# Decay sums of a gated recurrence: two levels in one product of 256 columns, with two sets of decayed queries and keys

## The chip, the cores and the metric

One core of one Trainium2 chip runs the whole kernel. The metric is the device time of one execution in microseconds (us). The kernel before took 1091.51 us, the median of 3 runs (1090.42 to 1091.56).

## The reference, cut to what matters

The program is two transformer blocks over 256 positions of width 1024: first attention with a retention branch and a feed-forward part, then a second block with a feed-forward part, a mixing part, cross attention to a memory, and another feed-forward part. Everything is float32. The change lies in the mixing part of the second block, in its gated recurrence (HGRN2) of 4 heads of 128 channels:

```python
def step(state, inp):                       # one chunk of positions
    qi, ki, vi, bi = inp                    # bi = cumulative sum of log f
    diff = bi[:, :, :, None, :] - bi[:, :, None, :, :]
    decay = jnp.exp(jnp.where(causal, diff, -jnp.inf))
    scores = jnp.einsum('bhtk,bhsk,bhtsk->bhts', qi, ki, decay)
    o = jnp.einsum('bhts,bhsv->bhtv', scores, vi) + \
        jnp.einsum('bhtk,bhkv->bhtv', qi * jnp.exp(bi), state)
    ...
```

With log f the logarithm of the forget gate, the score of position t with an earlier position s is the sum over the 128 channels of q[t] k[s] exp(sum of log f from s+1 to t). Beside it the mixing part projects its input to seven pieces of 512 columns (zf, zq, zi, zc, zu, zb, zg), convolves zc*zu over the positions, multiplies by zb, and projects both results back (w_out).

## The kernel before, in words

**Products of the projections.** TensorE rounds float32 operands in its fast mode, so every weight and every input is split into a high and a low part (w_hi, w_lo, hT_hi, hT_lo), and each product is three (function `three`, lines 1661 to 1663). The weights come in units of 128 x 2048. A unit passes through three rings of 3 slots: SyncE loads it (raw), ScalarE copies the high part (L583, `split_to`), VectorE subtracts to get the low part (L1056, `low_to`), TensorE uses it (`unit`: 24 products of 512 columns). ScalarE's copy waits until TensorE has used the unit three before it.

**The recurrence by levels.** The 256 positions are two blocks of 128. Inside a block the pairs (s, t) are sorted into 7 levels: at level l the block is cut into segments of 2^(l+1) positions, and the pairs with s in the early half and t in the late half of one segment belong to level l (LEVELS = 7). An eighth step, level 7, gives the pairs across the two blocks. For every level:

1. TensorE sums log f from each position to the middle of its segment: a product of logf_hi and logf_lo (128 positions x 128 channels, stationary) with a 0/1 matrix of 128 columns (`sums_r`, one matrix for each level), for 4 heads and 2 blocks: `decay_sums(level)`, L2073 and L2074. Block 0 goes to PSUM bank 4, block 1 to bank 7.
2. ScalarE takes the exponential into one of two buffers, `qk_dec[level % 2]` (the halves of `xn`): `level_decays(level)`, L949, 2 instructions of 128x512. The buffer is free when the pair scores of two levels ago have been made.
3. VectorE multiplies the late halves by the queries and the early halves by the keys: `decayed(level)`, L1541.
4. TensorE multiplies every head's 128x128 tile with itself: `pair_scores(level)`, L2092, 8 products. At level 7 it is 4 products into one bank ("cross", L2084).
5. VectorE keeps the pairs of this level by a mask: `keep_pairs`, L1529.

**The order of the work.** Each engine's order is written out by hand. On TensorE it is: transposes of queries and keys (L2063), `decay_sums(0)`, the pairs of a position with itself ("diag", L2114, 8 products), and then 8 steps. Step n computes unit n of the eight units of zc, zu, zb and zg, then `decay_sums(n + 1)`, then `pair_scores(n)`. At the end of step 5 it transposes zc*zu ("uT", L2100, into banks 2 and 3, which hold zb until ScalarE has copied it out), at the end of step 6 zb ("bT", the same line and banks). In the middle of step 7 stand the cross products. Then come the products with the values (L2143, L2146) and w_out, whose first half needs `conv_lo`, the low part of the convolution's result (L1594).

ScalarE's order here is: copies of the transposed queries (L963) and keys (L967), two weight copies, the zi piece (`streamed_out`, L646), and then in each of steps 0 to 7 one weight copy, `level_decays(step)` and what else is due: zc in step 1, zb in step 5, uT in step 6 (L983). After that come the two high parts of the convolution (L989), a weight copy, zg, and so on. VectorE in each level waits for both exponentials, runs `decayed`, `keep_pairs` of the level before, and a `low_to`; after level 6 comes the convolution (L1558, L1562), after level 7 the product with zb (L1569), the copy of the cross scores (L1581), a `low_to` and `conv_lo` (L1594).

**Banks.** `BankPlan` gives every use of a PSUM bank a name, in the order of use: `streamed` or `signalled` puts a fill on the list of its bank. `free(engine, name)` waits until every earlier fill of the bank has been read; `filled` waits until this one is written; `read_out` waits until this one has been read.

Of the kernel before, what the change touches and what calls it, by code (L numbers as in the profile page):

```python
# [32 lines left out]
ACT = mybir.ActivationFunctionType  # L33
AX = mybir.AxisListType

P = 128
# [157 lines left out]
def plan_banks():  # L194
# [85 lines left out]
    transposes("hkT", 2)  # L280
    for blk in range(TB):
        plan.signalled(("diag", blk), 5 + blk)
    for level in range(LEVELS):
        for blk in range(TB):
            plan.signalled(("decay", level, blk), [4, 7][blk])
            plan.signalled(("pairs", level, blk), 5 + blk)
        for step, name in ((LEVELS - 2, "uT"), (LEVELS - 1, "bT")):
            if level == step:
                plan.signalled(f"{name}0", 2)
                plan.signalled(f"{name}1", 3)  # L290
    for blk in range(TB):
        plan.signalled(("decay", LEVELS, blk), [4, 7][blk])
    plan.signalled("cross", 5)
    for blk in range(TB):
        plan.signalled(("hgrn", blk), [4, 7][blk])
# [26 lines left out]
def two_blocks_kernel(nc, io):  # L322
# [10 lines left out]
    with sems, stack:  # L333
# [122 lines left out]
        scT = carve(at, 8 * P); at += 1024  # L456
        crossT = carve(at, 4 * P); at += 512
        head_row = rows[:, 1, 0:512]
        lb_p = carve(at, 2, 512); lb = carve(at + 1024, 512); one_lb = carve(at + 1536, 512); at += 2048
        hgrn_sq = [lb_p[:, blk, :] for blk in range(TB)]  # L460
        level_mask = const2[:, (LEVELS + 2) * P:].rearrange("p (l t) -> p l t", t=P)
        qk_dec = [xn[:, b, :] for b in range(2)]


        mq = carve(0, TB, D)
# [21 lines left out]
        def filled(eng, name):  # L487

            b, _, s = plan.of[name]
            eng.wait_ge(bank_full[b], s + 1)  # L490
            return bank[b]

        def read_out(eng, name):

            b, k, _ = plan.of[name]
            eng.wait_ge(bank_read[b], k + 1)
# [7 lines left out]
        def read_sem(name):  # L504
            return bank_read[plan.of[name][0]]
# [72 lines left out]
        def _(act):  # L578
# [361 lines left out]
                for tb in range(TB):  # L940
                    copy_out((part, tb), dst[:, tb, :], func, scale=rstd[:, tb:tb + 1])

            def level_decays(level):
                for blk in range(TB):
                    b = filled(act, ("decay", level, blk))
                    if blk == 0 and level >= 2:

                        filled(act, ("pairs", level - 2, 1))
                    act.activation(qk_dec[level % 2][:, blk * 512:(blk + 1) * 512], b[:, :], ACT.Exp)\  # L949
                        .then_inc(read_sem(("decay", level, blk)), 1)  # L950

            streamed_out(0, "zf", fgate, ACT.Sigmoid)
            act.wait_ge(sem("fgate"), 1)
# [16 lines left out]
            for step in range(8):  # L970
                if step < LEVELS:
                    split_to(W_IN2 + 6 + step + RING)
                level_decays(step)
                if step == 1:
                    streamed_out(3, "zc", zc_sb)
                if step == 3:
                    split_to(W_IN2 + 10 + RING)
                if step == 5:
                    streamed_out(5, "zb", zb_sb)
                if step == LEVELS - 1:  # L980
                    for j in range(2):
                        b = filled(act, f"uT{j}")
                        act.activation(uT.rearrange("p (c t) -> p c t", t=T + 2)[:, 2 * j:2 * j + 2, 2:T + 2],  # L983
                                       b[:, :].rearrange("p (c t) -> p c t", t=T), ACT.Copy).then_inc(read_sem(f"uT{j}"), 1)
# [55 lines left out]
        def _(dve):  # L1040
# [490 lines left out]

            def decayed(level):

                buf = qk_dec[level % 2]
                for late, other in ((1, hqT), (0, hkT)):
                    h = 1 << level
                    v = buf.rearrange("p (n two h) -> p n two h", two=2, h=h)[:, :, late, :] if level < LEVELS else \
                        buf[:, late * 512:late * 512 + 512]
                    o = other.rearrange("p (n two h) -> p n two h", two=2, h=h)[:, :, late, :] if level < LEVELS else \
                        other[:, late * 512:late * 512 + 512]  # L1540
                    ins = dve.tensor_tensor(v, v, o, ALU.mult)  # L1541
                ins.then_inc(sem("level_decayed"), 1)
# [27 lines left out]
                                      b[:, :].rearrange("p (c t) -> p c t", t=T), ALU.mult).then_inc(read_sem(f"bT{j}"), 1)  # L1570

            for level in range(LEVELS + 1):
                read_out(dve, ("decay", level, 0))
                read_out(dve, ("decay", level, 1))
                decayed(level)
                if level:
                    keep_pairs(level - 1, ("pairs", level - 1))
                if level == LEVELS:
                    gated_convolution()
                    b = filled(dve, "cross")  # L1580
                    dve.tensor_copy(crossT, b[:, :]).then_inc(read_sem("cross"), 1)  # L1581
                low_to(W_IN2 + 9 + level)
                if level == LEVELS - 1:
                    convolution()
                if level == 4:

                    dve.wait_ge(split_used, W_IN2 + 10)
                    read_out(dve, ("zc", 1))
                    for tb in range(TB):
                        dve.scalar_tensor_tensor(out=zc_sb[:, tb, :], in0=bank_of(("zu", tb))[:, :], scalar=rstd[:, tb:tb + 1],  # L1590
                                                 in1=zc_sb[:, tb, :], op0=ALU.mult, op1=ALU.mult).then_inc(read_sem(("zu", tb)), 1)
# [66 lines left out]
        def _(pe):  # L1658
# [404 lines left out]
                        ins = pe.transpose(b[:, h * P:(h + 1) * P], src[:, blk, h * P:(h + 1) * P], ident)  # L2063
                    ins.then_inc(full_sem((name, blk)), 1)

            def decay_sums(level):

                for blk in range(TB):
                    b = free(pe, ("decay", level, blk))
                    m = sums_r[:, level + blk if level == LEVELS else level, :]  # L2070
                    for h in range(HG_HEADS):
                        o = b[:, h * P:(h + 1) * P]
                        pe.matmul(o, logf_hi[:, blk, h * P:(h + 1) * P], m, start=True, stop=False)  # L2073
                        ins = pe.matmul(o, logf_lo[:, blk, h * P:(h + 1) * P], m, start=False, stop=True)  # L2074
                    ins.then_inc(full_sem(("decay", level, blk)), 1)

            def pair_scores(level):

                pe.wait_ge(sem("level_decayed"), level + 1)
                buf = qk_dec[level % 2]  # L2080
                if level == LEVELS:
                    b = free(pe, "cross")
                    for h in range(HG_HEADS):
                        ins = pe.matmul(b[:, h * P:(h + 1) * P], buf[:, h * P:(h + 1) * P],  # L2084
                                        buf[:, 512 + h * P:512 + (h + 1) * P], start=True, stop=True)
                    ins.then_inc(full_sem("cross"), 1)
                    return
                for blk in range(TB):
                    b = free(pe, ("pairs", level, blk))
                    for h in range(HG_HEADS):  # L2090
                        v = buf[:, blk * 512 + h * P:blk * 512 + (h + 1) * P]
                        ins = pe.matmul(b[:, h * P:(h + 1) * P], v, v, start=True, stop=True)  # L2092
                    ins.then_inc(full_sem(("pairs", level, blk)), 1)
# [9 lines left out]

            pe.wait_ge(sem("sums_ready"), 1)
            pe.wait_ge(sem("logf_lo"), 1)
            decay_sums(0)
            for name in ("hqT", "hkT"):
                for q in range(2):
                    read_out(pe, (name, q))
            for blk in range(TB):  # L2110
                b = free(pe, ("diag", blk))
                for h in range(HG_HEADS):
                    s = slice(blk * 512 + h * P, blk * 512 + (h + 1) * P)
                    ins = pe.matmul(b[:, h * P:(h + 1) * P], hkT[:, s], hqT[:, s], start=True, stop=True)  # L2114
                ins.then_inc(full_sem(("diag", blk)), 1)
            parts = ["zc", "zu", "zb", "zg"]
            for step in range(8):
                k, half = step // 2, step % 2
                v = W_IN2 + 6 + step
                if half == 0:  # L2120
                    outs = [free(pe, (parts[k], tb)) for tb in range(TB)]
                h = 1 - half if parts[k] == "zg" else half
                unit(v, v + 1, [(hT_hi, hT_lo, tb, outs[tb]) for tb in range(TB)], range(4 * h, 4 * h + 4), 512,
                     half == 0, half == 1, {1: lambda: pair_scores(LEVELS)} if step == LEVELS else {})
                if step < LEVELS:
                    decay_sums(step + 1)
                    pair_scores(step)

                if step == LEVELS - 2:
                    read_out(pe, ("zu", 1))  # L2130
                    positions_last("uT", zc_sb)
                if step == LEVELS - 1:
                    read_out(pe, ("zb", 1))
                    positions_last("bT", zb_sb)
# [173 lines left out]
```

## Time and profile before

| | |
|---|---|
| median of 3 runs | 1091.51 us (1090.42 to 1091.56) |
| profiled execution | 1091.91 us, its span 1090.1 us |
| TensorE (PE) busy | 1035.2 us, 95% |
| VectorE (DVE) busy | 603.1 us, 55% |
| ScalarE (ACT) busy | 490.9 us, 45% |
| chain that ended last | PE 86%, DVE 7%, DMA 3%, ACT 2% |

The span runs from the first to the last profiled instruction. PEld is TensorE's weight load, which can lie beside a running product. The duration printed for one product includes its way through the array, so the pace of a row of products is read from the distance between their starts. "Idle before" is time in which the engine of the row did nothing just ahead of it, with what ended that.

### The profile page before, as it was taken

What the parts mean: (1) busy time and instruction counts of PE and PEld (TensorE: products, weight loads), DVE (VectorE), ACT (ScalarE), POOL (GpSimd) and SP (SyncE); (2) the same over time, 40 slices, a digit from 0 to 9 for tenths busy, and PEclk for the clock granted to TensorE, in tenths of its full rate; (3) what the DMA queues carried; (4) which work ended last, traced back from release to release, by engine and by line L of the source; (5) the groups of instructions that cost most, each with busy time, mean ns of one, the idle gap of its engine ahead of it and who ended that gap; (6) DMA issues with size and microseconds to landing.
All of it is one profiled execution on the core that took longest, in us unless ns stands there. A gap on an engine that the chain in (4) does not pass through costs nothing.

```text
span 1090.1 us, 13384 instructions
## 1 busy us (share of the span) xinstructions
PE 1035.2 (95%) x5212; PEld 843.4 (77%) x5212; DVE 603.1 (55%) x706; ACT 490.9 (45%) x581; POOL 0.2 (0%) x4
## 2 busy tenths in 40 slices
PE   4699999999999999999999999999999799999996
PEld 1477768887788888888888887788877578888885
DVE  1572665576755554475555545756775345555543
ACT  3343445536643444364444434653545335444531
POOL 0000000000000000000000000000000000000000
PEclk9799999999999999999999999999999899999998
DMA  9766473213455555545555555433235126545540
GB/s 373 282 237 260 171 298 117 78 40 114 177 175 194 188 188 188 192 176 204 191 188 189 171 193 216 174 136 116 88 144 193 39 78 230 175 173 192 193 155 38
DMA packets 26543, 188.71 MB, mean 173 GB/s; under 512 B 2945, under 2 KB 3201, under 8 KB 3969
## 3 DMA queue, kind: packets, MB, share of 16 engines
q1 hardware_dynamic: 25920, 185.63, 46.8%
q10 hardware_dynamic: 576, 2.43, 0.6%
q8 instruction: 34, 0.56, 0.2%
q14 instruction: 13, 0.10, 0.0%
HBM read 187.00 MB, written 1.05 MB: 173 GB/s over the span
## 4 chain that ended last, share of the span: by engine, by line
PE 86%; DVE 7%; DMA 3%; ACT 2%; issue 1%; SPq 0%; DVEq 0%; ACTq 0%
PE bank L1661 24%; PE bank L1663 24%; PE bank L1662 24%; DMA raw<-in_weights 3%; DVE w_lo L1056 2%; PE bank L1728 2%; PE bank L1889 1%; PE bank L1998 1%; PE bank L1717 1%; PE bank L1878 1%; ACT w_hi L583 1%; PE bank L2184 1%; PE bank L2092 1%; PE bank L2193 1%; PE bank L1928 1%
## 5 line engine op out<-in xcount | busy, mean ns | idle before, releaser
L1056 DVE TENSOR_TENSOR w_lo<-raw,w_hi 128x2048 fp32r<-128x2048 f32 (+1 forms) x151 | 338.9, 2248 | 278.2 <-ACT w_hi L583 278.1
L583 ACT ACTIVATE w_hi<-raw 128x2048 fp32r<-128x2048 f32 x148 | 283.1, 1916 | 277.6 <-PE bank L1663 249.6
L1661 PE MATMUL bank<-w_hi,hT_hi 128*128 128x512 f32 (+1 forms) x864 | 342.7, 397 | 5.7 <-issue 3.0
L1663 PE MATMUL bank<-w_hi,hT_lo 128*128 128x512 f32 (+1 forms) x864 | 336.8, 390 | 0.0
L1662 PE MATMUL bank<-w_lo,hT_hi 128*128 128x512 f32 (+1 forms) x864 | 336.3, 389 | 0.0
L1661 PEld LDWEIGHTS bank<-w_hi,hT_hi 128*128 128x128 f32 x864 | 163.4, 189 | 47.2 <-issue 9.6
L1663 PEld LDWEIGHTS bank<-w_hi,hT_lo 128*128 128x128 f32 x864 | 163.1, 189 | 34.4
L1662 PEld LDWEIGHTS bank<-w_lo,hT_hi 128*128 128x128 f32 x864 | 163.5, 189 | 32.1 <-issue 0.2
L1661 PE MATMUL bank<-w_hi,gT_hi 128*128 128x512 f32 x264 | 103.3, 391 | 0.0
L1663 PE MATMUL bank<-w_hi,gT_lo 128*128 128x512 f32 x264 | 102.8, 389 | 0.0
L1662 PE MATMUL bank<-w_lo,gT_hi 128*128 128x512 f32 x264 | 102.7, 389 | 0.0
L1663 PEld LDWEIGHTS bank<-w_hi,gT_lo 128*128 128x128 f32 x264 | 49.6, 188 | 10.4
L1662 PEld LDWEIGHTS bank<-w_lo,gT_hi 128*128 128x128 f32 x264 | 49.6, 188 | 10.2
L1661 PEld LDWEIGHTS bank<-w_hi,gT_hi 128*128 128x128 f32 x264 | 49.6, 188 | 10.0
L1728 PE MATMUL bank<-raw,silu_c 128*32 128x512 f32 x192 | 29.5, 715 | 19.7 <-DMA raw<-in_weights 19.7
L858 ACT ACTIVATE arena<-bank,rstd 128x256 f32<-128x256 f32 x44 | 18.4, 470 | 63.5 <-PE bank L1663 63.5
L1455 DVE SCALAR_TENSOR_TENSOR arena<-bank,rstd,arena 128x256 f32<-128x256 f32 x44 | 19.3, 479 | 30.8 <-ACT arena L858 30.8
L1728 PEld LDWEIGHTS bank<-raw,silu_c 128*32 128x32 f32 x192 | 4.7, 116 | 33.6 <-DMA raw<-in_weights 19.4
L1297 DVE TENSOR_REDUCE row_max<-bank 128x1 f32<-128x512 f32 (+1 forms) x24 | 14.4, 602 | 24.3 <-PE bank L1878 16.3
L1661 PE MATMUL bank<-memT_hi,w_hi 128*128 128x256 f32 x64 | 26.4, 412 | 0.0
L1443 DVE SCALAR_TENSOR_TENSOR x_res<-bank,x_res 128x512 f32<-128x512 f32 x16 | 10.3, 686 | 26.7 <-PE bank L1663 26.7
L1461 DVE TENSOR_TENSOR gT_lo<-bank,gT_hi 128x512 f32 (+1 forms) x33 | 22.8, 690 | 3.2
(261 smaller groups left out, 993.3 us busy)
## 6 DMA issues: line engine op xcount, KB each, us to landing
raw<-in_weights SPq DMA_DIRECT2D x172, 1024.0 KB, 4.7
arena<-in_const ACTq DMA_DIRECT2D x1, 1088.0 KB, 5.0
x_res<-in_x SPq DMA_DIRECT2D x1, 1024.0 KB, 8.3
arena<-in_ctx SPq DMA_DIRECT2D x1, 1024.0 KB, 9.9
memKT<-in_mem SPq DMA_DIRECT2D x1, 1024.0 KB, 10.3
out<-xn SPq DMA_DIRECT2D x2, 512.0 KB, 2.7
arena<-in_const SPq DMA_DIRECT2D x1, 770.0 KB, 6.3
rows<-in_final_norm ACTq DMA_DIRECT2D x1, 512.0 KB, 5.1
```

Source lines behind the costliest of these rows:

```text
L583: act.activation(w_hi[:, v_slot, :], raw[:, u_slot, :], ACT.Copy).then_inc(hi_ready, 1)
L858: act.activation(gate[:, c % 3, tb, :], bank[(c % 3) * 2 + tb][:, 0:256], ACT.Silu, scale=rstd[:, tb:tb + 1] if f else 1.0)\
L1056: ins = dve.tensor_tensor(w_lo[:, v_slot, n], raw[:, u_slot, n], w_hi[:, v_slot, n].bitcast(F32), ALU.subtract)
L1297: chain(dve.reduce_max(row_max[:, s:s + 1], b[:, 0:n], AX.X))
L1455: dve.scalar_tensor_tensor(out=g, in0=bank[b][:, 256:512], scalar=rstd[:, tb:tb + 1] if f else 1.0, in1=g, op0=ALU.mult, op1=ALU.mult).the ...
L1461: dve.tensor_tensor(gT_lo[:, s, :], bank[6][:, :].rearrange("p (a t) -> p a t", t=T), gT_hi[:, s, :].bitcast(F32), ALU.subtract).then_inc( ...
L1661: pe.matmul(out, hi, rhi, start=start, stop=False)
L1662: pe.matmul(out, hi, rlo, start=False, stop=False)
L1663: return pe.matmul(out, lo, rhi, start=False, stop=stop)
L1717: ins = pe.transpose(b[:, e * T + tb * P:e * T + (tb + 1) * P], src[:, tb, (2 * q + e) * P:(2 * q + e + 1) * P], ident)
L1728: ins = pe.matmul(b[32 * j:32 * j + 32, :], silu_c[:, k, :], raw[:, u % RING, 512 * j:512 * j + 512], start=(k == 0), stop=(k == MOD_K - 1))
L1878: pe.matmul(b[:, :], qaT[:, j, tb * P:(tb + 1) * P], kaT[:, kv, :], start=True, stop=True).then_inc(full_sem(("scores", s)), 1)
```

## The change

Eight times 16 products of 128 columns become eight times 8 products of 256 columns: two neighbouring matrices of `sums_r` are the moving operand of one product. `decay_sums(p, blk)` now makes the sums of levels 2p and 2p+1 of one block, two heads in each bank (bank 4 for heads 0 and 1, bank 7 for heads 2 and 3). The second set of decayed queries and keys (`dec_set`) lies in the arena where the bounds of the forget gate lay; each set holds two levels.

```diff
+    for p in range((LEVELS + 1) // 2):
+        for blk in range(TB):
+            for hp in range(2):
+                plan.signalled(("decay", p, blk, hp), [4, 7][hp])
     for level in range(LEVELS):
         for blk in range(TB):
-            plan.signalled(("decay", level, blk), [4, 7][blk])
             plan.signalled(("pairs", level, blk), 5 + blk)
...
-    for blk in range(TB):
-        plan.signalled(("decay", LEVELS, blk), [4, 7][blk])
...
-        lb_p = carve(at, 2, 512); lb = carve(at + 1024, 512); one_lb = carve(at + 1536, 512); at += 2048
+        dec_set = carve(at, 2, 1024); lb_p = carve(at, 2, 512); lb = carve(at + 1024, 512); one_lb = carve(at + 1536, 512); at += 2048
...
-        qk_dec = [xn[:, b, :] for b in range(2)]
+        dec_sets = [xn[:], dec_set]
+        qk_dec = lambda level: dec_sets[level // 2 % 2][:, level % 2, :]
...
-            def level_decays(level):
-                for blk in range(TB):
-                    b = filled(act, ("decay", level, blk))
-                    if blk == 0 and level >= 2:
-
-                        filled(act, ("pairs", level - 2, 1))
-                    act.activation(qk_dec[level % 2][:, blk * 512:(blk + 1) * 512], b[:, :], ACT.Exp)\
-                        .then_inc(read_sem(("decay", level, blk)), 1)
+            def level_decays(p, blk):
+                for hp in range(2):
+                    b = filled(act, ("decay", p, blk, hp))
+                    if blk == 0 and hp == 0 and p >= 2:
+                        filled(act, ("pairs", 2 * p - 3, 1))
+                    at = blk * 512 + hp * 256
+                    act.activation(dec_sets[p % 2][:, :, at:at + 256].rearrange("p l (h t) -> p h l t", t=P),
+                                   b[:, :].rearrange("p (h l t) -> p h l t", l=2, t=P), ACT.Exp)\
+                        .then_inc(read_sem(("decay", p, blk, hp)), 1)
...
-                level_decays(step)
+                if step == 0:
+                    level_decays(0, 0)
+                    level_decays(0, 1)
+                elif step < LEVELS:
+                    level_decays((step + 1) // 2, (step - 1) % 2)
...
-                read_out(dve, ("decay", level, 0))
-                read_out(dve, ("decay", level, 1))
+                if level % 2 == 0:
+                    for blk in range(TB):
+                        for hp in range(2):
+                            read_out(dve, ("decay", level // 2, blk, hp))
...
-            def decay_sums(level):
-
-                for blk in range(TB):
-                    b = free(pe, ("decay", level, blk))
-                    m = sums_r[:, level + blk if level == LEVELS else level, :]
-                    for h in range(HG_HEADS):
-                        o = b[:, h * P:(h + 1) * P]
-                        pe.matmul(o, logf_hi[:, blk, h * P:(h + 1) * P], m, start=True, stop=False)
-                        ins = pe.matmul(o, logf_lo[:, blk, h * P:(h + 1) * P], m, start=False, stop=True)
-                    ins.then_inc(full_sem(("decay", level, blk)), 1)
+            def decay_sums(p, blk):
+
+                m = sums_r[:, 2 * p:2 * p + 2, :]
+                if 2 * p + 1 == LEVELS and blk:
+                    m = sums_r[:, 2 * p:2 * p + 3:2, :]
+                for hp in range(2):
+                    b = free(pe, ("decay", p, blk, hp))
+                    for e in range(2):
+                        o = b[:, e * 2 * P:(e + 1) * 2 * P].rearrange("p (l t) -> p l t", t=P)
+                        d = slice((2 * hp + e) * P, (2 * hp + e + 1) * P)
+                        pe.matmul(o, logf_hi[:, blk, d], m, start=True, stop=False)
+                        ins = pe.matmul(o, logf_lo[:, blk, d], m, start=False, stop=True)
+                    ins.then_inc(full_sem(("decay", p, blk, hp)), 1)
...
-            decay_sums(0)
+            decay_sums(0, 0)
             for name in ("hqT", "hkT"):
...
                 ins.then_inc(full_sem(("diag", blk)), 1)
+            decay_sums(0, 1)
...
                 if step < LEVELS:
-                    decay_sums(step + 1)
+                    if step < LEVELS - 1:
+                        decay_sums((step + 2) // 2, step % 2)
                     pair_scores(step)
```

## Rows read from the trace of the kernel before

**Rows 1.** The page: busy time of the engines, and the chain of waits by engine.
```profile
PE 1035.2 (95%) x5212; PEld 843.4 (77%) x5212; DVE 603.1 (55%) x706; ACT 490.9 (45%) x581; POOL 0.2 (0%) x4
PE 86%; DVE 7%; DMA 3%; ACT 2%; issue 1%; SPq 0%; DVEq 0%; ACTq 0%
```
**Rows 2.** Groups of instructions by line and form: the decay sums.
```profile
L2074 PE MATMUL bank<-sums_r,logf_lo 128*128 128x128 f32 x64 | 14.7, 276 | 0.0
L2073 PE MATMUL bank<-sums_r,logf_hi 128*128 128x128 f32 x64 | 14.4, 268 | 0.0
```
**Rows 3.** Timeline of TensorE: start, duration (us), instruction, count.
```profile
710.92 0.31 PE L2073 MATMUL bank<-sums_r,logf_hi 128*128 128x128 f32 x1
...
712.74 2.00 PE L2114 MATMUL bank<-arena 128*128 128x128 f32 x16
714.49 0.48 PE L1661 MATMUL bank<-w_hi,hT_hi 128*128 128x512 f32 x1
...
720.02 0.22 PE L2073 MATMUL bank<-sums_r,logf_hi 128*128 128x128 f32 x1
...
721.76 2.00 PE L2092 MATMUL bank<-xn 128*128 128x128 f32 x16
...
765.39 0.22 PE L2073 MATMUL bank<-sums_r,logf_hi 128*128 128x128 f32 x1
```
**Rows 4.** Timeline of TensorE where products of 256 columns run in a row.
```profile
162.08 0.28 PE L1661 MATMUL bank<-memT_hi,w_hi 128*128 128x256 f32 x1
...
162.44 0.28 PE L1661 MATMUL bank<-memT_hi,w_hi 128*128 128x256 f32 x1
```
**Rows 5.** Timeline of ScalarE around the first exponentials.
```profile
710.71 1.09 ACT L967 ACTIVATE arena<-bank 128x512 f32<-128x512 f32 x2 [0.26 <-PE bank L2063]
711.69 3.71 ACT L583 ACTIVATE w_hi<-raw 128x2048 fp32r<-128x2048 f32 x2
715.30 1.26 ACT L646 ACTIVATE arena<-bank,rstd 128x512 f32<-128x512 f32 x2
716.57 1.28 ACT L949 ACT_TABLE_LOAD   x1
717.87 1.09 ACT L949 ACTIVATE xn<-bank 128x512 f32<-128x512 f32 x2
```
**Rows 6.** Timeline of ScalarE and VectorE from unit 5's end to w_out.
```profile
765.65 1.91 ACT L583 ACTIVATE w_hi<-raw 128x2048 fp32r<-128x2048 f32 x1 [6.19 <-PE bank L1663]
767.47 1.25 ACT L646 ACTIVATE arena<-bank,rstd 128x512 f32<-128x512 f32 x2
...
769.79 1.30 DVE L1541 TENSOR_TENSOR xn<-xn,arena 128x512 f32<-128x512 f32 x2 [5.51 <-ACT xn L949]
...
779.43 1.29 DVE L1541 TENSOR_TENSOR xn<-xn,arena 128x512 f32<-128x512 f32 x2
...
782.58 1.23 ACT L989 ACTIVATE hT_hi<-arena 128x512 fp32r<-128x512 f32 x2 [3.20 <-DVE arena L1569]
783.71 1.90 ACT L583 ACTIVATE w_hi<-raw 128x2048 fp32r<-128x2048 f32 x1
...
787.85 1.29 DVE L1594 TENSOR_TENSOR hT_lo<-arena,hT_hi 128x512 fp32r<-128x512 f32 x2
```
**Rows 7.** Timeline of TensorE: the cross products and the start of w_out.
```profile
782.56 1.05 PE L2084 MATMUL bank<-xn 128*128 128x128 f32 x8
...
789.20 0.50 PE L1661 MATMUL bank<-w_hi,hT_hi 128*128 128x512 f32 x1 [0.16 <-DVE hT_lo L1594]
```
**Rows 8.** Windows: busy time and count by engine, granted clock, DMA share, GB/s.
```profile
284.00:288.00 4.00, 2.24 (x10) 1.58 (x9) 3.78 (x8) 1.65 (x3) 0.00 (x0) 1.00 0.61 246
...
668.00:672.00 4.00, 3.09 (x22) 2.40 (x20) 1.87 (x4) 1.45 (x5) 0.00 (x0) 1.00 0.47 133
672.00:676.00 4.00, 2.82 (x7) 2.28 (x8) 4.00 (x8) 2.61 (x7) 0.00 (x0) 0.69 0.85 342
676.00:680.00 4.00, 4.00 (x17) 3.27 (x16) 2.15 (x4) 1.69 (x2) 0.00 (x0) 0.89 0.51 145
```

More of the change, by code:

```diff
@@ L1532, in decayed @@
             def decayed(level):
-                buf = qk_dec[level % 2]
+                buf = qk_dec(level)
                 for late, other in ((1, hqT), (0, hkT)):
@@ L2064, in _ @@
                     ins.then_inc(full_sem((name, blk)), 1)
-            def decay_sums(level):
-                for blk in range(TB):
-                    b = free(pe, ("decay", level, blk))
-                    m = sums_r[:, level + blk if level == LEVELS else level, :]
-                    for h in range(HG_HEADS):
-                        o = b[:, h * P:(h + 1) * P]
-                        pe.matmul(o, logf_hi[:, blk, h * P:(h + 1) * P], m, start=True, stop=False)
-                        ins = pe.matmul(o, logf_lo[:, blk, h * P:(h + 1) * P], m, start=False, stop=True)
-                    ins.then_inc(full_sem(("decay", level, blk)), 1)
+            def decay_sums(p, blk):
[10 more added lines that the diff above has]
+                    ins.then_inc(full_sem(("decay", p, blk, hp)), 1)
             def pair_scores(level):
                 pe.wait_ge(sem("level_decayed"), level + 1)
-                buf = qk_dec[level % 2]
+                buf = qk_dec(level)
                 if level == LEVELS:
```

## The prediction

> **What bounds the kernel.** I read the page first, then the groups by line, then the timelines of the stretch that the change touches. TensorE is busy for 1035.2 us of the 1090.1 us span and makes up 86% of the chain that ended last [rows 1]. So a microsecond taken off TensorE's queue is a microsecond off the time, unless TensorE then waits for something. The whole question is where in this stretch it would wait, and the timelines answer it. The profiled execution took 1091.91 us, 0.4 above the median of the runs shown (1091.51). I sum against the first and take 0.4 off at the end.
>
> **What the decay sums cost now.** They are 128 products (64 and 64) [rows 2]. Their printed durations overlap, so I take distances between starts. After unit 0, 16 of them stand between 720.02 and the pair scores at 721.76: 1.74 us, about 0.11 each. The first group takes 1.82 (710.92 to 712.74) [rows 3]. TensorE doesn't pause between them, so all eight groups, 1.82 + 7 x 1.74 = 14.0 us, are on its queue.
>
> **What they cost after.** 64 products of 256 columns. Such products run elsewhere in this kernel: three of them between 162.08 and 162.44, 0.12 each [rows 4]. A group of 8 is then 0.96 us, and each group saves 0.78. Bounds for the new product: not below the 0.11 of the one with half the columns (group 0.88, saving 0.86), and not above 0.23, the product of 512 columns, which is 24 in a unit: 714.49 to 720.02 is 5.53 us [rows 3] (group 1.84, saving -0.10). The row of the same width decides, 0.96. The one group whose moving operand is two matrices with a third between them has no row of its own; it comes behind unit 5 and, as shown below, does not count.
>
> The Trainium skill ("TensorE: Matmul & The Clock Gate", section "Back-to-back issue gap") gives about 81 ns for one product of 128 columns in a stream with its weight loads and about 131 ns for 512. An estimate from that page for 256 columns, on a straight line between, is 98 ns; a group would go from 1.30 to 0.78 us and save 0.51. The trace has 110 and 230 ns for the two ends [rows 3], so the measurement disagrees and decides.
>
> **The start: a new wait.** This is the step that matters most. Before, level 0's two blocks went to banks 4 and 7, and both banks were free. Now block 0 fills both banks (heads 0 and 1, heads 2 and 3), and block 1 needs both again. `decay_sums(0, 1)` stands on TensorE's queue ahead of unit 0, and `free` makes it wait until ScalarE has taken the exponential of block 0 out of bank 4. When is that? ScalarE's queue before its first exponential holds the key copies, two weight copies (711.69, 3.71 us), zi (715.30) and a table load (716.57); the first exponential starts at 717.87 [rows 5]. None of these waits for anything that the change brings forward: they run back to back. Two exponentials take 1.09 us, the first alone 0.6, so bank 4 is read at about 718.5 and bank 7 at 719.0.
>
> TensorE's side: block 0 from 710.92 takes 0.96 and the first group's extra 0.08, to 711.95. The diagonal products need the key copies, which end at 711.80 (710.71 + 1.09), so they hardly wait; they take 1.75 (712.74 to 714.49) and end at about 713.7. Then TensorE stands still until 718.5, for 4.8 us. Four products into bank 4, then four into bank 7, which is free at 719.0: unit 0 starts at about 719.5 in place of 714.49 [rows 3, 5]. That is 5.0 us late, and everything behind it on the queue (unit 0, all pair scores, all later units) is late with it.
>
> Bounds of this wait: if the exponential, which now writes four runs of 128 in place of one of 512, keeps its time, it is 5.0. The nearest row is the same instruction with the plain layout; I see no reason for a gain, and if a run cost it half as much again, bank 7 would be free 0.5 later, so 5.0 to 5.5. I take 5.0.
>
> **Steps 0 to 4.** Behind each of units 0 to 4 a group of 8 replaces one of 16: 5 x 0.78 = 3.9 us won. On the new times no wait comes due here. Pair scores of level 0 need the exponentials of both blocks (to about 720.4) and 1.3 us of VectorE; TensorE asks for them when unit 0 and a group have passed, 719.5 + 5.5 + 1.0 = 726.0. Not late. From there on ScalarE's exponentials of one block follow each group as before, two 128x512 instructions in each step, and VectorE's two levels come from sums that are complete one step earlier or at the same step as before. Before unit 5 nothing gets late.
>
> So unit 5 ends at 765.39 + 5.0 - 3.9 = 766.5, that is 1.1 us later than now.
>
> **From unit 5's end to w_out: nothing is won.** Behind it two groups go (the one of level 7 wholly, another one halved), 1.74 + 0.78 = 2.5 us of TensorE's queue. But w_out starts at 789.20, after a wait for the low part of the convolution [rows 7], and that comes from a chain of ScalarE and VectorE which begins at unit 5's end: weight copy 765.65, zb 767.47, exponentials, VectorE's `decayed` at 769.79, mask, low part, convolution, `decayed` of level 7 at 779.43, product with zb, ScalarE's high parts at 782.58, weight copy 783.71, VectorE's low part, and the low part of the convolution at 787.85 [rows 6]. From 765.39 to 789.20 it is 23.8 us with hardly a gap, and the change leaves every instruction of it where it is (two exponentials behind zb, as now). TensorE will wait inside this stretch. The transposes of zc*zu need the banks of zb, read out at 768.72 (3.3 behind unit 5's end), and TensorE comes there after 0.96 + 1.75 = 2.7: 0.6 of waiting. The cross products need `decayed` of level 7, done at 780.72, 15.3 behind; they start now at 782.56, 17.2 behind [rows 6, 7]. The remaining 2.1 us or so are waited before w_out. So w_out starts 1.1 us late as well, and the rest of the kernel, whose order is the same, shifts by 1.1.
>
> **The clock.** Where TensorE did little before 673, the granted clock fell: 1.00, then a mean of 0.69 and of 0.89 over two stretches of 4 us [rows 8]. Its levels are full (2.4 GHz) and half (1.2 GHz), so it was half for (0.31 + 0.11) x 4 x 2 = 3.4 us, which cost TensorE about 1.7 us of work. In the stretch 668 to 672 TensorE was still busy for 3.09 of 4 us, and 2.82 of the next 4. The new wait of 4.8 us without any product is a longer pause than any there. I expect the clock to fall once and take 1.7 us. Bounds: 0 (it stays up), and 3.4 (twice as long at half).
>
> The Trainium skill ("TensorE: Matmul & The Clock Gate", section "HAM oscillation — how this bites in real kernels") says that a wait between two bursts of products throws the gate back to half rate, and that the fall is paid at every such wait. By it the time is the 1.7 us case. The trace agrees with it around 673 and not at 284 to 288 [rows 8]. By the rule alone the second new pause, of 2.1 us before w_out, would be a risk too.
>
> **Sum.** 1091.91 + 5.0 - 3.9 + 0 + 1.7 = 1094.7; less 0.4 for the median: 1094.3 us, slower by 0.26%.
>
> **The rivals.**
>
> *The clock stays up.* The same without the 1.7: 1092.6. For it: between 284 and 288 TensorE was idle for about 1.8 of 4 us and the clock stayed at 1.00 [rows 8], so not every pause is punished. Against: that pause is much shorter than 4.8 us. It would count as no change.
>
> *It falls twice.* The pause before w_out (2.1 us, behind light products of 128 columns) brings a second fall, or the first lasts longer: 1094.3 + 1.7 = 1096.0. For it: around 673, where the clock fell, the pauses were no longer. Against: the one at 284 to 288 is about as long and cost nothing [rows 8].
>
> *No new wait at the start.* If banks 4 and 7 were free for block 1, because ScalarE reads them earlier, unit 0 would start at about 714.7 and the pair scores of level 0 would wait 0.4 for four exponentials in a row. Then 0.6 - 3.9 = -3.3 us, 1088.2: faster. The decision falls at 713.7: the first exponential would have to end by then, 4.8 us sooner than now, and the table load and zi ahead of it stand in [rows 5]. Nothing in the trace shows this.
>
> *TensorE's work is all that counts.* Then 14.0 - 8 x 0.96 = 6.3 us are won, 1085.2. Against: both waits above, of the new one and that of [rows 6].
>
> *The 256-column products are slow.* Group 1.84: nothing won, and 5.0 + 0.5 + 1.7 late: 1098.7. Against: [rows 4].
>
> **Chances.** Forecast (new wait, one fall of the clock) 0.50; clock stays up 0.20; two falls 0.17; no wait or TensorE alone 0.08; slow products or later exponentials 0.05. A measurement of this kernel tells a change from none at about 0.2%, which is 2.2 us: slower begins at 1093.7. The forecast lies 0.6 us beyond it, and as the length of the half-rate stretch varies, about a quarter of its chance ends below. So slower: 0.37 + 0.17 + 0.05 = 0.59; same: 0.13 + 0.20 = 0.33; faster: 0.08. The range takes in the clock's bounds and both neighbours, 1091.6 to 1096.8; it leaves out the faster cases, the slow products and the corners.
>
> **What would show each step.** In the new trace: TensorE idle for 4.8 us between the diagonal products and the second group of sums, released by ScalarE's first exponential; unit 0 starting near 719.5; products of sums 0.12 apart; unit 5's end near 766.5 plus the clock's share; the distance from there to the start of w_out 23.8 us, with idle time of TensorE at the transposes of zc*zu, the cross products and w_out; a granted clock of 0.5 just after 718. The prediction is wrong if unit 0 starts near 714.7, if the distance of 23.8 shrinks, or if the clock holds.

## The result and the profile after

The changed kernel took 1094.69 us (median of 6 runs, 1092.64 to 1096.5), the kernel before 1091.24 (6 runs, 1089.76 to 1091.56): ratio 1.0030, 95% interval 1.0018 to 1.0042. A second set (12 runs of the changed kernel, 29 of the kernel before) gave 1093.95 against 1090.55, ratio 1.0030 (1.0018 to 1.0043). One execution in the experiments below was disturbed (5886 us) and is left out of its median. Slower by 0.3%, though TensorE has 5.3 us less to do (1035.2 in [rows 1], 1029.9 now). Below, times inside the stretch are counted from the first product of the decay sums, since the two profiled executions reach it 0.24 us apart (710.92 and 710.68).

The page of the kernel after, busy time and the chain by engine; and the row of granted clock in 40 slices, which for the kernel before was `9799999999999999999999999999999899999998`:

```profile
PE 1029.9 (94%) x5148; PEld 837.0 (77%) x5148; DVE 602.7 (55%) x706; ACT 490.8 (45%) x581; POOL 0.2 (0%) x4
...
PEclk9799999999999999999999999999999999999999
...
PE 85%; DVE 7%; ACT 3%; DMA 3%; issue 1%; SPq 0%; DVEq 0%; ACTq 0%
```

ScalarE's part of the chain rose from 2% to 3%. The groups by line and form answer to [rows 2]: half the products, twice the columns, and a wait of 4.4 us that wasn't there.

```profile
L2085 PE MATMUL bank<-sums_r,logf_hi 128*128 128x256 f32 x32 | 8.9, 306 | 4.4 <-ACT xn L951 4.4
L2086 PE MATMUL bank<-sums_r,logf_lo 128*128 128x256 f32 x32 | 8.7, 299 | 0.0
```

TensorE's timeline after, answering to [rows 3] and [rows 7]:

```profile
710.68 0.36 PE L2085 MATMUL bank<-sums_r,logf_hi 128*128 128x256 f32 x1
...
711.81 2.02 PE L2126 MATMUL bank<-arena 128*128 128x128 f32 x16
718.27 0.58 PE L2085 MATMUL bank<-sums_r,logf_hi 128*128 128x256 f32 x1 [4.44 <-ACT xn L951]
...
720.15 0.63 PE L1670 MATMUL bank<-w_hi,hT_hi 128*128 128x512 f32 x1
...
726.12 0.28 PE L2085 MATMUL bank<-sums_r,logf_hi 128*128 128x256 f32 x1
...
727.07 1.95 PE L2104 MATMUL bank<-xn 128*128 128x128 f32 x16
...
767.24 0.28 PE L2085 MATMUL bank<-sums_r,logf_hi 128*128 128x256 f32 x1
...
783.60 1.13 PE L2096 MATMUL bank<-arena 128*128 128x128 f32 x8 [1.47 <-DVE arena L1536]
...
791.27 0.50 PE L1670 MATMUL bank<-w_hi,hT_hi 128*128 128x512 f32 x1 [1.11 <-DVE hT_lo L1603]
```

TensorE stands still behind the diagonal products until ScalarE has taken the exponential out of the bank. Unit 0 starts 9.47 us behind the first sums (720.15 - 710.68) where it was 3.57 [rows 3]. A group of sums takes 0.95 (726.12 to 727.07), and w_out starts at 80.59 in place of 78.28: 2.3 us late. ScalarE at the same place, answering to [rows 5]:

```profile
716.33 1.28 ACT L951 ACT_TABLE_LOAD   x1
717.62 1.08 ACT L951 ACTIVATE xn<-bank 128x512 f32<-128x512 f32 x2
719.53 0.60 ACT L951 ACTIVATE xn<-bank 128x512 f32<-128x512 f32 x1 [0.82 <-PE bank L2086]
720.39 0.60 ACT L951 ACTIVATE xn<-bank 128x512 f32<-128x512 f32 x1 [0.26 <-PE bank L2086]
```

An exponential with the new layout takes 0.60 us. One with the plain layout took as long in the kernel before:

```profile
776.38 0.60 ACT L949 ACTIVATE xn<-bank 128x512 f32<-128x512 f32 x1 [5.70 <-PE bank L2074]
```

The clock (windows, columns as in [rows 8]) fell in the wait:

```profile
712.00:716.00 4.00, 1.84 (x16) 1.64 (x15) 2.61 (x2) 4.00 (x4) 0.00 (x0) 1.00 0.00 0
716.00:720.00 4.00, 1.73 (x8) 1.73 (x9) 0.92 (x2) 3.15 (x5) 0.00 (x0) 0.72 0.75 262
720.00:724.00 4.00, 4.00 (x17) 3.29 (x17) 2.88 (x3) 0.73 (x2) 0.00 (x0) 0.85 0.02 4
```

From unit 5's end to w_out the chain of [rows 6] stands as it was: weight copy, zb, and at its end the high part of the convolution, two weight copies, and the low part:

```profile
767.50 1.91 ACT L585 ACTIVATE w_hi<-raw 128x2048 fp32r<-128x2048 f32 x1 [5.34 <-PE bank L1672]
769.32 1.25 ACT L648 ACTIVATE arena<-bank,rstd 128x512 f32<-128x512 f32 x2
...
784.66 1.23 ACT L996 ACTIVATE hT_hi<-arena 128x512 fp32r<-128x512 f32 x2 [10.63 <-DVE arena L1576]
785.80 3.70 ACT L585 ACTIVATE w_hi<-raw 128x2048 fp32r<-128x2048 f32 x2
...
789.93 1.28 DVE L1603 TENSOR_TENSOR hT_lo<-arena,hT_hi 128x512 fp32r<-128x512 f32 x2
```

It took 24.0 us (767.24 to 791.27) after 23.8 before.

The two profiled executions differ by 0.7 us only (1092.64 and 1091.91), less than the 2.3 by which w_out is late. The rows of granted clock show why: slice 32 (about 845 to 872 us) has 8 before and 9 after. The clock fell twice there in the profiled execution of before and once in that of after, and from w_out to the end it is 300.9 us before and 299.4 after. The second profile of the changed kernel has 8 in that slice and 300.4 us. Whether this goes with the kernel is open. All five profiles in which the clock stayed up through the first pause or had no such pause (before, filled wait, exponentials first, exponentials first with three moves, before with two moves) have 300.7 to 300.9 us behind w_out. Of the six in which it fell at the start, five have 299.1 to 299.4. So a fall at the start may be followed by one fall fewer here; no experiment tried that.

### The profile page after: what moved, and what is told of

It is laid out like the page before. It is cut to its first block, busy times and chain, and to the rows that moved or that the text cites. A ratio compares the mean times of both kernels' runs of the same rounds, so it can differ in the third digit from the quotient of the medians.

```text
span 1090.7 us, 13252 instructions
## 1 busy us (share of the span) xinstructions
PE 1029.9 (94%) x5148; PEld 837.0 (77%) x5148; DVE 602.7 (55%) x706; ACT 490.8 (45%) x581; POOL 0.2 (0%) x4
## 4 chain that ended last, share of the span: by engine, by line
PE 85%; DVE 7%; ACT 3%; DMA 3%; issue 1%; SPq 0%; DVEq 0%; ACTq 0%
PE bank L1670 24%; PE bank L1672 24%; PE bank L1671 24%; DMA raw<-in_weights 3%; DVE w_lo L1063 2%; PE bank L1737 2%; ACT w_hi L585 2%; PE bank L1898 1%; PE bank L2007 1%; PE bank L1726 1%; PE bank L1887 1%; PE bank L2104 1%; PE bank L2207 1%; PE bank L2198 1%; PE bank L1937 1%
```

## The experiments

Each was timed in five rounds beside the kernel before on the same chip; the groups of runs used different chips, so differences between two rows are best taken through each row's own time before. The last column of the table counts in each profile from the first decay sum to the start of w_out, which leaves out what the clock does elsewhere.

| kernel | median us | before us | ratio (95%) | to w_out |
|---|---|---|---|---|
| before | | | | 78.28 |
| changed | 1094.69 | 1091.24 | 1.0030 (1.0018 to 1.0042) | 80.59 |
| changed, again | 1093.95 | 1090.55 | 1.0030 (1.0018 to 1.0043) | 81.94 |
| wait alone | 1095.83 | 1090.86 | 1.0051 (1.0038 to 1.0065) | 83.77 |
| products of 128 | 1099.59 | 1090.86 | 1.0074 (1.0060 to 1.0088) | 85.86 |
| filled wait | 1091.57 | 1090.86 | 1.0004 (0.9995 to 1.0013) | 79.27 |
| exponentials first | 1086.81 | 1090.86 | 0.9962 (0.9949 to 0.9976) | |
| the same, again | 1088.20 | 1090.56 | 0.9977 (0.9963 to 0.9990) | 74.77 |
| two moves in the tail | 1093.00 | 1090.55 | 1.0021 (1.0012 to 1.0031) | 81.00 |
| three moves in the tail | 1090.52 | 1090.56 | 0.9999 (0.9985 to 1.0014) | 77.76 |
| exponentials first, three moves | 1085.05 | 1090.55 | 0.9945 (0.9930 to 0.9960) | 71.85 |
| before with two moves | 1090.64 | 1090.55 | 0.9996 (0.9987 to 1.0005) | 78.14 |

**The wait alone**, put into the kernel before:

```diff
+            read_out(pe, ("decay", 0, 0))
             parts = ["zc", "zu", "zb", "zg"]
```

> The kernel before with one more wait: TensorE, between the diagonal products and unit 0, waits until the exponential of level 0, block 0 has been taken. Theory A (the new wait at the start is what the change costs, and the clock falls in it): unit 0 starts at about 718.6 in place of 714.49, 4.1 us late, the clock falls once and takes about 1.4 more, nothing of it is made good later: 1091.2 + 5.5 = 1096.7 us. Rival B (a wait here is made good further on, and the change is slow for another reason, such as the wider products or the new layout of the exponentials): 1091 to 1092.

It came out as theory A has it: 5.0 us slower in the medians and 5.5 to w_out (83.77 - 78.28). Unit 0 starts 7.60 behind the first sums in place of 3.57, so 4.0 of this is the pause and 1.5 the slow clock. TensorE's waits in that profile hold one long entry, and nothing of it is made good on the way to w_out:

```profile
PE bank L1661 <- ACT xn L949: 3.8, 1, 3.8
```

**The products split**, in the changed kernel:

```diff
-                        pe.matmul(o, logf_hi[:, blk, d], m, start=True, stop=False)
-                        ins = pe.matmul(o, logf_lo[:, blk, d], m, start=False, stop=True)
+                        for l in range(2):
+                            pe.matmul(o[:, l, :], logf_hi[:, blk, d], m[:, l, :], start=True, stop=False)
+                            ins = pe.matmul(o[:, l, :], logf_lo[:, blk, d], m[:, l, :], start=False, stop=True)
```

> The changed kernel, each product of 256 columns made as two of 128 into the same places; every wait and bank as in the changed kernel. Theory A (a group of 16 takes 0.85 us more than one of 8, and only what stands ahead of unit 5's end counts): five groups behind units 0 to 4 and part of the group before unit 0, 5 x 0.85 + 0.6 = 4.9 us slower than the changed kernel, 1094.7 + 4.9 = 1099.6. Rival C (all of TensorE's work counts): 8 x 0.85 = 6.8 slower, 1101.5. Rival B (the wide products bring nothing): 1094.7.

1099.59, 4.9 above the changed kernel's 1094.69: what theory A names, and 1.9 short of rival C. Taken against each one's own time before, it is 5.3 (8.7 slower and 3.4 slower). To w_out it is 85.86, also 5.3 more than the first profile of the changed kernel. The groups behind unit 5 cost nothing: from unit 5's end to w_out it is 24.03 us with either width.

**The wait filled** with products, in the changed kernel:

```diff
+            spare = free(pe, ("zc", 0))
+            for _ in range(18):
+                pe.matmul(spare[:, :], hT_hi[:, 0, 0:P], hT_hi[:, 0:2, :].rearrange("p a t -> p (a t)"), start=True, stop=True)
             decay_sums(0, 1)
```

> The changed kernel with 18 products of 512 columns put into the wait ahead of the second group of sums, into a bank that unit 0 starts afresh; their result is not used. 18 x 0.23 = 4.1 us fit into the wait of 4.4. Theory A: the granted clock stays at 1.00 around 718, unit 0 starts about 0.9 earlier and runs at full pace, 1.4 us less than the changed kernel: 1093.3. Rival D (the clock's part is nothing, all of the loss is the pause): 1094.7, and the clock falls as well or its fall costs nothing.

TensorE's timeline in this kernel:

```profile
713.47 4.37 PE L2130 MATMUL bank<-hT_hi 128*128 128x512 f32 x18
718.15 0.38 PE L2085 MATMUL bank<-sums_r,logf_hi 128*128 128x256 f32 x1 [0.32 <-ACT xn L951]
...
719.22 0.40 PE L1670 MATMUL bank<-w_hi,hT_hi 128*128 128x512 f32 x1
```

Windows, columns as in [rows 8]:

```profile
716.00:720.00 4.00, 3.68 (x21) 2.90 (x20) 0.81 (x2) 3.63 (x6) 0.00 (x0) 1.00 0.74 262
720.00:724.00 4.00, 4.00 (x20) 3.30 (x19) 3.85 (x4) 0.02 (x1) 0.00 (x0) 1.00 0.00 0
```

The second group of sums starts at the same place (7.60 behind the first, 7.59 in the changed kernel), so the pause is as long; only the clock is different, and it stays up. To w_out it is 79.27: 1.3 less than the first profile of the changed kernel and 2.7 less than the second. The time fell by more than the expected 1.4: the ratio went from 1.0030 to 1.0004, some 2.8 us, though the two intervals leave room for half of that. In the second profile of the changed kernel the clock was at half for longer:

```profile
716.00:720.00 4.00, 3.00 (x11) 2.80 (x12) 0.16 (x1) 2.62 (x5) 0.00 (x0) 0.50 0.62 250
720.00:724.00 4.00, 4.00 (x13) 3.10 (x13) 4.00 (x5) 0.00 (x0) 0.00 (x0) 0.65 0.00 0
```

**The exponentials of block 0 first**, in the changed kernel:

```diff
+            level_decays(0, 0)
             streamed_out(2, "zi", hv)
...
                 if step == 0:
-                    level_decays(0, 0)
                     level_decays(0, 1)
```

> The changed kernel with the two exponentials of level 0 and 1, block 0 moved on ScalarE ahead of the two weight copies and zi, so that banks 4 and 7 are read at about 714. Theory A: TensorE no longer stands still before unit 0, which starts near 714.8; the clock stays up; pair scores of level 0 wait 0.3 to 0.5 us for the exponentials of block 1, which come behind zi; five groups are won at 0.85: 1091.2 + 0.3 + 0.4 - 4.25 = 1087.7 us. Rival C (all of TensorE's work counts, 6.6 us): 1084.8. Rival B (the wide products or the new layout cost something of their own): not under 1090.

1086.81, near theory A's 1087.7. For a readable profile it ran once more:

> The same kernel as with the exponentials of block 0 first, for a profile at full pace. Theory A: the stall before unit 0 is gone, unit 0 starts 3.7 to 4.0 us behind the first sums, the clock stays at 1.00 there, steps of 8.22 us; from unit 5's end to w_out 24.0 us as in the changed kernel, with 1.1 and 1.5 us of TensorE's waits in it. Time 1086.9, 3.9 less than before.

ScalarE's first exponentials in this profile, behind the table load, which moved with them,

```profile
710.66 1.28 ACT L951 ACT_TABLE_LOAD   x1
711.95 1.09 ACT L951 ACTIVATE xn<-bank 128x512 f32<-128x512 f32 x2
```

and TensorE's:

```profile
709.76 0.36 PE L2085 MATMUL bank<-sums_r,logf_hi 128*128 128x256 f32 x1
...
712.67 0.36 PE L2085 MATMUL bank<-sums_r,logf_hi 128*128 128x256 f32 x1
...
713.71 0.40 PE L1670 MATMUL bank<-w_hi,hT_hi 128*128 128x512 f32 x1
```

No pause is left ahead of unit 0: block 1's sums follow at 712.67, unit 0 starts 3.95 behind the first sums, and w_out at 74.77, 3.5 earlier than in the kernel before. The median, 1088.20, is 2.4 under that of before, where the first set of runs gave 4.0; both intervals lie under 1.

**Two moves in the tail** of the changed kernel: ScalarE copies a weight unit earlier, VectorE makes the low part of the convolution before that unit's low part.

```diff
             load_table(ACT.Silu)
+            split_to(W_OUT2 + 2)
...
-                low_to(W_IN2 + 9 + level)
+                if level < LEVELS:
+                    low_to(W_IN2 + 9 + level)
```

> The changed kernel with two moves behind unit 7: ScalarE copies the weights of w_out's second unit ahead of the high part of the convolution, and VectorE makes the low part of the convolution ahead of the low part of those weights. Theory A (what TensorE saves behind unit 5 is given back in waits for a chain of ScalarE and VectorE): the wait of 1.1 us before w_out goes, the wait of 1.5 before the cross products stays: 1.1 us less than the changed kernel. Rival E (these waits are not on the path, the time is lost elsewhere): no change.

1.0 us less in the medians (1093.00 and 1093.95), as theory A says; the intervals of the two ratios overlap, so the medians alone would not carry it. The profile does. From unit 5's end to w_out it is 22.93 us in place of 24.03, and TensorE's wait before w_out is gone while the others stand. (To w_out from the first sums it is 81.00, not less than 80.59, because here the clock was at half about as long at the start as in the second profile of the changed kernel.)

```profile
PE bank L2087 <- ACT xn L951: 4.4, 1, 4.4
PE bank L2098 <- DVE arena L1537: 1.4, 1, 1.4
PE bank L2074 <- ACT arena L966: 0.3, 1, 0.3
```

> The kernel before with the two moves behind unit 7 alone. Theory A (in the kernel before TensorE arrives at w_out when the chain is ready, and waits only 0.2 us): 0.2 us less than before, which can't be told from no change. If the moves won 1 us here as well, the wait was there before the change and is not its savings given back.

1090.64 against 1090.55: nothing, as expected. In the kernel before TensorE had its own work until w_out could start, so the wait is the change's savings given back.

**Three moves in the tail**: the third puts zb and the last exponentials ahead of a weight copy.

```diff
                 if step == 5:
-                    streamed_out(5, "zb", zb_sb)
+                    used(W_IN2 + 11)
+                    for tb in range(TB):
+                        copy_out(("zb", tb), zb_sb[:, tb, :], scale=rstd[:, tb:tb + 1])
+                    level_decays(3, 1)
+                    split_to(W_IN2 + 12 + RING)
```

> The changed kernel with all three moves of the tail and the wait at the start left in. Theory A: both waits behind unit 5 (1.5 and 1.1 us) and the 0.2 at the transposes go: 2.8 less than the changed kernel, 3.4 - 2.8 = 0.6 more than the kernel before, 1091.3. Rival E (the wait before the cross products hides other waits, and only the last one counts): as with the two moves alone, 1.0 less than the changed kernel.

80.59 to w_out becomes 77.76, 2.8 less, and the time is that of the kernel before. From unit 5's end to w_out it is 21.08 us. Of the waits in this stretch only the first is left, 4.4 us. Rival E, by which it would be as with the two moves alone (22.93), is out.

**All together:**

> The exponentials of block 0 first on ScalarE (as in the run before), the two moves behind unit 7, and one more in step 5: ScalarE copies zb and takes the last exponentials ahead of a weight copy. Theory A: all the places where TensorE waits in this stretch are gone but some 0.4 us at the pair scores of level 0; against the kernel before 8 x 0.85 - 0.4 = 6.4 us less, 1084.5, and 2.8 less than with the exponentials first alone. Rival E (the tail's waits are not on the path): as with the exponentials first alone, 1086.9.

1085.05 us, ratio 0.9945: 5.5 us faster than the kernel before and the best version of the study. To w_out it is 71.85, 6.4 less than 78.28, just the sum that was expected. TensorE waits for nothing from the decay sums to w_out; its only entry among the waits comes from ahead of them:

```profile
PE bank L2078 <- ACT arena L966: 0.3, 1, 0.3
```

## Why the prediction was right

- **The new wait at the start.** Right in place, releaser and size: TensorE idle 4.44 us (forecast 4.8) until ScalarE's first exponential. Forecast without the clock: unit 0 at 719.5, 8.6 behind the first sums. With the clock kept up it was 8.67 (filled wait). The wait alone costs 5.0 to 5.5 us, and taking it away turns the change from 3.4 us slower to 2.4 to 4.0 faster.
- **The price of a product.** 0.12 from [rows 4], and 0.12 measured; a group takes 0.95. A step, though, became 0.85 shorter, not 0.78: from 9.07 ((765.39 - 720.02) / 5 in [rows 3]) to 8.22 ((767.24 - 726.12) / 5). Some 0.04 of it are the pair scores behind the group, 1.71 in place of 1.75. The estimate of 0.51 won for a group, from the figures of the Trainium skill ("TensorE: Matmul & The Clock Gate", section "Back-to-back issue gap"), was wrong: a group went from 1.74 to 0.95, 0.79 less.
- **The net before the clock.** Forecast 1.1 us late at unit 5's end and at w_out. In the filled wait, where the clock stays up, it is 0.8 at unit 5's end (55.24 behind the first sums, 54.47 before) and 79.27 - 78.28 = 1.0 at w_out. That the second fits so closely is partly luck: the steps won 0.3 more than forecast (5 x 0.85 in place of 3.9), and the stretch behind them took 0.2 more.
- **Nothing won behind unit 5.** Right: 24.0 us against 23.8. But the waits in it were shared out wrongly. Forecast: 0.6 us at the transposes of zc*zu, none at the cross products, 2.1 before w_out. Measured: about 0.2, 1.47 and 1.11. The cross products came 16.4 us behind unit 5's end, not 15.3, since they also need bank 5, which VectorE's mask of level 6 reads (L1536 in the row of 783.60). It cost nothing, because the chain to w_out ended later still. The 0.2 more stand on VectorE from the start of the convolution on, where it pauses for 0.52 us behind its own memset (L1559); why the pause is longer than before was not followed up.
- **The clock.** The fall was forecast as one, at 1.7 us. Against the filled wait it cost 1.3 in one profile of the changed kernel (80.59 - 79.27) and 2.7 in the other (81.94 - 79.27), in both at the pause and nowhere else in the stretch. The clock was at half for 3.4 us in the first, as forecast: (0.28 + 0.15) x 4 x 2. In the second it was twice that, the upper bound of the forecast. No second fall came at the pause before w_out. The prediction called that pause a risk by the rule of the Trainium skill ("TensorE: Matmul & The Clock Gate", section "HAM oscillation — how this bites in real kernels"). But the waits in the example there are longer than the bursts of products before them. On short pauses the traces here show both outcomes. Before, the clock fell behind pauses of 0.55 and 1.53 us around 673 and stayed up behind one of 1.76 between 284 and 288; after, it stayed up behind the 1.47 and the 1.11. The term was somewhat small: the sum said 2.8 us slower, the medians say 3.4. That the forecast of 1094.3 came within 0.4 us of the median is luck in part: its clock term alone is 1.3 in one execution and 2.7 in another.

The rivals: that the clock stays up is what the filled wait made true by hand, 1091.57, and not what the kernel does. That it falls twice or for longer (1096.0) is right for some executions, as the second profile shows: one fall, twice as long. That all of TensorE's work counts (6.3 us) is wrong for the changed kernel and right for the version without the waits, which gains 5.5 us in the medians and 6.4 to w_out.

## What to carry to other kernels

When one fill of a bank is split over two, or two stages share what one had, write down for every bank who reads it and what stands ahead of the reader on its queue; the saved work is worth nothing if the reader comes later. Behind a shortened engine look for the chain that runs beside it: here it used up everything that was saved in the last 24 us until three pieces of work had changed places. Both faults were of order alone, and cost more than the new products won.

## What the runs showed of the hardware

A product of 128 columns at half clock takes as long as one of 256. TensorE's timeline of the kernel with products of 128, where the clock fell at about 721.9:

```profile
721.63 0.27 PE L2087 MATMUL bank<-sums_r,logf_lo 128*128 128x128 f32 x1
721.74 0.27 PE L2086 MATMUL bank<-sums_r,logf_hi 128*128 128x128 f32 x1
721.85 0.32 PE L2087 MATMUL bank<-sums_r,logf_lo 128*128 128x128 f32 x1
721.97 0.42 PE L2086 MATMUL bank<-sums_r,logf_hi 128*128 128x128 f32 x1
722.18 0.42 PE L2087 MATMUL bank<-sums_r,logf_lo 128*128 128x128 f32 x1
722.40 0.73 PE L1670 MATMUL bank<-w_hi,hT_hi 128*128 128x512 f32 x1
```

The granted clock is 1.00 up to 721.9, 0.53 from there to 722.6 and 0.50 behind it. The distance goes from 0.11 to 0.21. In the changed kernel at half clock the products of 256 columns stand 0.21 apart as well, where at full clock it is 0.12:

```profile
719.08 0.41 PE L2086 MATMUL bank<-sums_r,logf_lo 128*128 128x256 f32 x1
719.29 0.41 PE L2085 MATMUL bank<-sums_r,logf_hi 128*128 128x256 f32 x1
```

So what bounds the small product doubles with the slower clock. The Trainium skill ("TensorE: Matmul & The Clock Gate", section "LDWEIGHTS (loading the stationary operand)") gives the weight load a time by its columns alone, 128 / 1.2 = 107 ns, with no word of the clock; at full clock that agrees with the 0.11, at half clock a load of 107 ns would not hold the products 0.21 apart. That the load is what takes the time was not tried by itself.

A pause of 4.4 us cost 1.3 us of slow products in one execution and 2.7 in another of the same kernel, with the products and the pause in the same places. In all six profiles with such a pause (3.8 to 4.4 us) and no products in it the clock was at half for either 3.4 us (four of them) or 6.9 us (the second of the changed kernel, and the one with two moves in the tail). The runs of the changed kernel lie within 1090.81 and 1097.11.
